# Hybrid S5 and DeltaNet layer: where the projection units stand among the levels of the triangular inverse

## The reference, cut to what matters

```python
kk = jnp.einsum('nbhid,nbhjd->nbhij', kc, kc)
lower = jnp.where(strict, bc[..., :, None] * kk * decay, 0.0)
tmat = lax.linalg.triangular_solve(eye + lower, eye, left_side=True, lower=True)
u = tmat @ (vc * bc[..., None])
w = tmat @ (kc * (bc * jnp.exp(gc))[..., None])
```

## Time and profile before

| | |
|---|---|
| median of three runs | 2059.02 us (2058.67 to 2062.05) |
| profiled execution | 2060.37 us |
| span in its trace | 2058.3 us |
| mean granted TensorE clock | 0.992 |
| busy: TensorE, VectorE, ScalarE, GpSimd | 97%, 54%, 40%, 14% |
| first inverse in the trace | level 0 at 467 us, last half ends at 524.4 us |
| second inverse | level 0 at 563 us, last half ends at 619.6 us |

### The profile page before, as it was taken

The page is one execution under the profiler, slowest core; times in us unless marked ns, Lnnn a source line. Parts: engine busy times, 40 slices in busy tenths (PEclk is TensorE's granted clock), DMA queues, the critical chain, the costliest instruction groups (busy, mean ns, idle before and its releaser), DMA issues.

```text
span 2058.3 us, 40224 instructions
## 1 busy us (share of the span) xinstructions
PE 2006.8 (97%) x16339; PEld 1961.1 (95%) x16339; DVE 1115.3 (54%) x1393; ACT 830.6 (40%) x1089; POOL 288.9 (14%) x372
## 2 busy tenths in 40 slices
PE   8899999988999999999999999999999999999998
PEld 7899999888889979999999999999999999999998
DVE  6799887644444477754444444433444444444554
ACT  7333335762333346244433333333333333333543
POOL 3854442000001110011000000000000000010110
PEclk9999999999999999999999999999999999999999
DMA  7544444443345577654444444444444444444443
GB/s 186 174 147 124 137 136 142 130 118 97 106 124 147 165 231 234 230 171 151 148 149 153 144 152 156 141 154 148 152 146 152 148 147 153 138 153 148 149 149 102
DMA packets 299646, 310.24 MB, mean 151 GB/s; under 512 B 24770, under 2 KB 290067, under 8 KB 299219
## 3 DMA queue, kind: packets, MB, share of 16 engines
q1 hardware_dynamic: 295844, 296.76, 46.9%
q0 software_dynamic: 3264, 11.64, 2.0%
q10 hardware_dynamic: 418, 0.12, 0.0%
HBM read 291.34 MB, written 17.14 MB: 150 GB/s over the span
## 4 chain that ended last, share of the span: by engine, by line
PE 90%; DVE 5%; ACT 2%; issue 1%; DMA 1%; SPq 0%; ACTq 0%; DVEq 0%
PE pg L2101 83%; DVE wlo L1379 2%; DVE cacc L1708 1%; ACT whi L924 1%; PE side_a L2144 1%; PE side_a L2135 1%; DMA raw<-in_w_out 0%; PE side_a L2436 0%; PE side_a L2101 0%; PE side_b L2144 0%; DMA xtok<-in_x_sample 0%; PE side_a L2455 0%; PE side_a L2413 0%; PE side_b L2397 0%; PE side_b L2101 0%
## 5 line engine op out<-in xcount | busy, mean ns | idle before, releaser
L1379 DVE TENSOR_TENSOR wlo<-raw,whi 128x1024 fp32r<-128x1024 f32 (+1 forms) x528 | 649.5, 1237 | 702.7 <-ACT whi L924 701.3
L924 ACT ACTIVATE whi<-raw 128x1024 fp32r<-128x1024 f32 (+1 forms) x528 | 545.2, 1039 | 923.3 <-PE pg L2101 885.3
L2101 PE MATMUL pg<-xhi,whi 128*128 128x320 f32 x2816 | 884.1, 314 | 28.0 <-DVE wlo L1379 28.0
L2101 PE MATMUL pg<-xhi,wlo 128*128 128x320 f32 x2816 | 874.1, 310 | 0.0
L2101 PE MATMUL pg<-xlo,whi 128*128 128x320 f32 x2816 | 874.1, 310 | 0.0
L2101 PEld LDWEIGHTS pg<-xhi,whi 128*128 128x128 f32 x2816 | 532.1, 189 | 37.5 <-DVE wlo L1379 22.2
L2101 PEld LDWEIGHTS pg<-xlo,whi 128*128 128x128 f32 x2816 | 532.3, 189 | 0.8
L2101 PEld LDWEIGHTS pg<-xhi,wlo 128*128 128x128 f32 x2816 | 532.0, 189 | 0.0
L2101 PE MATMUL pg<-mlo,whi 128*128 128x320 f32 x704 | 217.4, 309 | 0.0
L2101 PE MATMUL pg<-mhi,wlo 128*128 128x320 f32 x704 | 217.4, 309 | 0.0
L2101 PE MATMUL pg<-mhi,whi 128*128 128x320 f32 x704 | 217.4, 309 | 0.0
(11 more groups left out here) (486 smaller groups left out, 1896.4 us busy)
## 6 DMA issues: line engine op xcount, KB each, us to landing
raw<-in_w_in SPq DMA_DIRECT2D x144, 512.0 KB, 4.0
raw<-in_w_gate SPq DMA_DIRECT2D x88, 512.0 KB, 3.5
raw<-in_w_up SPq DMA_DIRECT2D x88, 512.0 KB, 3.5
raw<-in_w_down SPq DMA_DIRECT2D x80, 512.0 KB, 3.4
raw<-in_w_out SPq DMA_DIRECT2D x32, 512.0 KB, 3.4
raw<-in_w_ple_gate SPq DMA_DIRECT2D x32, 512.0 KB, 3.4
raw<-in_w_a SPq DMA_DIRECT2D x16, 512.0 KB, 5.6
raw<-in_w_b SPq DMA_DIRECT2D x16, 512.0 KB, 4.3
```

The costliest lines, as they stand in the source:

```text
L924: act.activation(whi[:, r, 0:nk, :], raw[:, r, 0:nk, :], ACT.Copy).then_inc(w_hi, 1)
L1379: dve.tensor_tensor(wlo[:, r, 0:nk, :], raw[:, r, 0:nk, :], whi[:, r, 0:nk, :].bitcast(F32), ALU.subtract).then_inc(w_lo, 1)
L2101: ins = pe.matmul(out[:, m, 0:N], w, a, start=first and k == 0 and part == 0, stop=last and k == nk - 1 and part == 2)
```

## The change

It alters the numbers of units in two lines of the slot list, for the prompt chunks alone. The first product of every level but 0 has no unit behind it; the halves of levels 1 to 4 have two, those of levels 5 and 6 keep one. Both inverses keep 11 units in their slots.

```diff
         for k in range(LEVELS[c]):
-            slot([("m1", c, k)], 0 if c < 2 and k in (2, 4) else 1)
+            slot([("m1", c, k)], 0 if c < 2 and k else 1)
             if k:
-                slot([("tab", c, k)], 1)
+                slot([("tab", c, k)], 2 if c < 2 and k < 5 else 1)
```

## The result

The changed kernel took 2086.16 us (median of four runs, 2083.48 to 2087.84) against 2060.14 (2058.67 to 2062.05): a ratio of 1.0125, 95% interval 1.0107 to 1.0142, so about 26 us slower. Its profiled execution took 2085.84 us, with a span of 2083.8. The forecast was 2081.6, in a range from 2074 to 2090.

What follows compares the result with a forecast made beforehand. TensorE, busy 97% of the span, was taken as the bound. Waits of 17.9 us plus 4.7 us of slow clock made 22.6 us, which on the median of 2059.0 gave 2081.6 us, range 2074 to 2090.

Steps and rivals of the forecast that it cites:

- The direction and the mechanism: Both prompt inverses: slower (chance 0.95), as TensorE waits for the copy and for weights of a unit not split ahead.
- The waits: TensorE's added waits at levels 1, 3, 5 and 6 of both inverses: 6.4 + 7.4 + 4.0 = 17.9 us.
- levels 1 and 3: Stretch from first product to next unit grows from 1.93 to 3.53 us: 1.60 each, 6.4 us for four.
- level 5: Stretch grows from 2.83 to 6.55 us as ScalarE's copies precede the next split: 3.72 each, 7.4 for two inverses.
- level 6: Stretch grows from 2.14 to 4.16 us: 2.02 each, 4.0 us for two inverses.
- levels 2 and 4: Still no unit between first product and halves, one more behind the halves: stretch unchanged, no gain.
- The second unit behind the halves: Levels 1 to 4: covers VectorE's subtractions, which one unit covers already with 3.2 us to spare; gain nothing.
- The clock: Falls of about 1.56 us: one behind each level 5, one in four new short stretches, none at level 6; 4.7 us.
- The first: Rival: the clock falls at every stretch without a unit, 35.1 us in sum, so 2094; chance 0.06.
- The second: Rival: levels 5 and 6 pay only what levels 1 and 3 pay, 12.8 us, so 2072; chance 0.06.
- Giving back later: Rival: a later wait not tied to TensorE's progress shrinks by the same 18 us, 2059 to 2064; chance 0.02.
- The fourth: Rival: weights split ahead, ScalarE's high part before the copy, end the present empty-slot waits; 8.0 us gained, 2051; chance 0.02.

Runs made afterwards that it cites:

- e3: The changed kernel, with ScalarE and VectorE splitting the first unit behind the halves ahead of their first-product steps (levels 1 to 6); 2063.6 us, ratio 1.0022 to before.
- e9: The kernel before, with only levels 1 and 3 changed (no unit behind their first product), sample inverse left alone; 2066.0 us, ratio 1.0034.
- e10: The kernel before, with only levels 5 and 6 changed (no unit behind their first product), sample inverse left alone; 2077.4 us, ratio 1.0091.
- e6: The changed kernel, with ScalarE's six corner and diagonal copies of level 5 moved behind the split of the next unit; 2076.7 us, ratio 1.0080 to before.
- e5: The kernel before, with ScalarE and VectorE splitting the first unit behind the halves ahead of their first-product steps (levels 1 to 6); 2055.0 us, ratio 0.9978.
- e11: The changed kernel, with unread identity matmuls in TensorE's waits behind the halves (4 at levels 1-4, 16 at 5, 5 at 6); 2082.1 us, ratio 1.0114 to before.
- e2: The kernel before, with only levels 5 and 6 changed, but also two units behind some halves of the sample inverse; 2083.0 us, ratio 1.0106.
- e4: The changed kernel, with more unread identity matmuls behind the halves (7 at levels 1-4, 29 at 5, 9 at 6); 2092.8 us, ratio 1.0152 to before.
- e1: The kernel before, with only levels 1 and 3 changed, but also two units behind some halves of the sample inverse; 2075.7 us, ratio 1.0074.

## Why the prediction was right

**The direction and the mechanism** held: slower, because the split of the next unit queues behind the copy on ScalarE. e3 shows it by taking the queueing away.

**The waits.** Forecast 17.9 us, by the one trace of the changed kernel 18.3: levels 1 and 3 cost 1.51, 1.51, 1.51 and 1.68 (1.60 forecast), level 5 3.71 and 3.70 (3.72), level 6 2.03 and 2.12 (2.02), and levels 2 and 4, forecast at nothing, 0.5 in sum through a pause that went and one that came. e9 and e10 show the two parts add up.

**The second unit behind the halves** was put at nothing, and it did a little: two units in a row take 3.60 us each where a single one between side steps takes 3.7 (the earlier trace rows and the row at 488.51). Over both inverses 1.2 us.

**The clock** was the term that was too small: 4.7 us forecast, 8.9 measured, less 1.2 for the pairs and 0.4 for all other work. That is the miss, and two things make it up. Behind a level 5 the next unit took 5.93 and 6.02 us, at a clock of 0.58 and 0.57 where 0.67 had been forecast, so 2.3 us each and not the 1.56 read off and the earlier trace rows. The wait before it, 3.87 us, was a little longer than the longest in the trace of before, 3.59. And two waits that are in both kernels, 2.17 us behind level 0 and 1.9 us before the second chunk's kk products, were followed by falls this time (5.13 and 5.12 us), 3.0 us that I had put at nothing because the one trace of before showed none. The short stretches behaved as forecast, two falls among the eight (behind level 3 of the first and level 4 of the second inverse), and level 6 had none. The traces of the other kernels make the falls at those two waits a matter of chance: of the twelve that have the level-0 wait, four have the slow unit behind it in the first inverse and none in the second, and of the thirteen that have the 1.9 us wait, seven have it there. So these 3.0 us are a matter of luck, which another execution need not have. What decides whether the clock falls behind such a wait stays open.

**The rivals.** The first, a fall at every empty slot, is out with two of eight short ones. The page TensorE: Matmul & The Clock Gate of the Trainium skill, section "A second HAM failure mode: psum-queue depth-cycling", makes the swing a matter of frequent short idles; this trace doesn't agree for the short stretches, and the two long ones, with 3.87 us of idle time in one piece, are not what it describes. The second, level 5 no dearer than the others, is out by the 6.54 us, and e6 shows the copies as its cause. Giving back later did not happen: the rest of the span changed by 0.4 us. The fourth, a gain from splits ahead, needs another order on ScalarE than the change has; e5 shows that with that order it is real, at 4.5 us rather than 8.

Outside the forecast were TensorE's pauses without a releaser, which moved the times of e3, e5 and e11 by 3 to 5 us each. They were in the earlier trace rows already, inside the 3.84 us stretch; the last section says what the traces show of them.

## What to carry to other kernels

Where engines work through one list of slots, an empty slot takes away not only TensorE's cover but also the preparation of the next unit, which then queues behind the slot's copies: price the chain from the end of the first product to the next unit, copy by copy, and not only the copy that the next step needs. If a slot has to be empty, put the split ahead of the copy on the engines that prepare, or leave empty the slot after which the preparing engine has nothing to wait for. The longest waits here cost more than their length, through the clock, and a price read from one trace for whether it falls at all is a sample of one.

## What the runs showed of the hardware that had not been expected

TensorE's clock was at its lower level for longer behind the longest waits. The six units behind an unfilled level 5 (the changed kernel, e2 and e10, each with a wait of 3.87 us) took 5.9 to 6.4 us at a mean of 0.54 to 0.58; the two of e6, behind a wait of 1.24 us in a stretch of 3.9, took 5.25 at 0.67. With the wait filled by matmuls whose result nobody reads, the next unit ran at the full level in all four places of e4 and e11 (3.7 us at 1.00). In two of the four the clock fell nevertheless, while the added matmuls ran.

TensorE paused for 0.5 to 2.4 us at a time with no releaser in the profile ("issue"). Between 450 and 660 us the fourteen traces have 34 such pauses, in the runs of 32 x 32 matmuls at a level with no unit between, in the added matmuls, or in a unit close behind. Every kernel, the one before too, had some. They were hidden where the wait for the weights was as long anyway, and cost 3.6 us in two levels of e3, where it was not.

The traces point to the delivery of TensorE's instructions. The page of every kernel has a DMA queue for instructions, in packets of 16 KB; this is its line for the changed kernel (packets, MB, share of the DMA engines):

```profile
q8 instruction: 90, 1.47, 0.3%
```

Each of the 34 pauses ends 1.25 to 1.54 us after one of these packets has landed, though of all matmuls between 470 and 640 us only 6% start 1.2 to 1.6 us behind the latest landing. Waits of 1.7 to 3.2 us before the state updates (L2413, behind 730 us), for which the profile names no releaser either, don't have this mark: in the traces of the kernel before, the change, e1, e2 and e9 they end 3.6 to 18 us after a landing. TensorE also stops at the same few places in its program: with 5548 matmuls behind it in seven of the traces and with 6057 in eight, and where two stops of one kernel follow closely, as in the changed kernel, e1, e3, e4, e6 and e11, they are 254 or 255 matmuls apart. No run changed how the instructions come in, so this is read from the traces and not shown by an experiment.
